# Masked position tables for the sparse attention branch, made by GpSimd ahead of time, in place of mask products on TensorE

## The chip, the cores and the metric

One core of a Trainium2 chip runs the whole kernel in one launch. The metric is device time in microseconds of one execution, the median of several. The engines are TensorE (PE in the rows, with PEld for its weight loads), VectorE (DVE), ScalarE (ACT), GpSimd (POOL) and SyncE (SP, which here only issues DMAs). Each has its own instruction queue that runs in order, and they wait for each other on semaphores.

## The reference, cut to what matters

The kernel computes one decoder layer for 512 tokens of width 1024: a shared input projection, three attention branches whose outputs are merged by gates, an output projection, and a SwiGLU. The change lies in branch A, sparse attention with 8 heads, of which this is the core:

```
score = einsum('bqh,bqhs->bqs', wi, relu(einsum('bqhd,bsd->bqhs', qi, k_idx)))
score = where(key_pos <= q_pos, score, -inf)
_, sel = top_k(score, 128)                      # one choice of keys for all 8 heads
bias = bias_tab[rel_bucket(q_pos - sel)]        # one column per head
logits = q_lat . kv_lat[sel] * ATTN_SCALE + bias
p = softmax(where(dist >= 0, logits, -inf))
```

The kernel gathers nothing. It computes the products with all visible keys and pushes the keys that were not chosen out by a large number. For the first 128 queries every visible key is chosen, so that only the query blocks 1, 2 and 3 (with 256, 384 and 512 keys, together 1152 columns) need a mask.

## The kernel before, in words

**The stages around the change.** An indexer makes `score` [128, 1152]. DVE then takes the 128 largest of each row away in rounds (`select_keys`), and one DVE instruction turns what is left into `key_mask`: 1e30 where a key is not chosen, 0 where it is (line 2042, semaphore `mask_ready`). Behind it comes the attention stage, a hand-written schedule of 88 steps `v`. Steps 0 to 31 are the dilated branch (C), steps 32 to 63 branch A, steps 64 to 79 the differential branch (B). In branch A step v = 32 + 4h + i is head h (0 to 7), query block i (0 to 3), with 128(i+1) keys. The 88 steps are mixed on TensorE with dense projections (`project`, lines 877 to 879, and the `bv` products, lines 1247 to 1249), so that TensorE has work while the other engines turn a step's scores into probabilities.

**One step.** PE writes logits, with the sign turned, into a PSUM bank (`scores`). DVE adds the position table and takes the row minimum in one instruction (`shift`, line 2065, semaphore `shifted`). ACT takes the exponential (line 1605, `exped`). DVE takes the reciprocal of the row sum (line 2083), POOL scales (line 808, `normed`), PE transposes (line 1153), ACT copies (line 1617, `pt_ready`), PE multiplies with the values (lines 1177, 1182, 1185). Steps are begun in pairs: at an even v DVE and PE take v and v+1. PE may only begin the scores of step k once step k-2 is shifted (line 1110), since there are two banks.

**The mask.** The logits of a step of branch A are two products on PE (lines 1128 and 1129) and, for i > 0, a third one: the identity `ident_r` times the columns of `key_mask` of this block, added into the same bank (line 1135).

**The tables.** For each head a table [128, 512] in SBUF holds the bias by distance, with 1e30 where a key lies ahead of the query. It is a Toeplitz read of `rep_dram`, 128 copies of a row in DRAM (`toeplitz`). SP loads them into two buffers `tab[0]` and `tab[1]` in turn (line 670), in its loop over n. The order of SP's queue matters here: at n = 0 and 1 the two tables of heads 0 and 1 are issued one behind the other, and only then `keys_twice(0)` and `keys_twice(1)` (line 654), each two DMAs that copy 64 rows of the keys of a pair of heads into the other 64 partitions. `keys_twice(t)` waits for ACT, which writes the keys of pair t at step KEY_STEPS[t] (26 and 35 for the first two; line 1679). At n = 2 SP first stores and reloads the dilated outputs `o_far` (lines 667 and 669), then loads the table of head 2.

**POOL** has nothing to do between line 802 (`rep_dram`) and step 31.

**ACT** makes `ident_r` at step 24 (line 1662), and the split queries `aq_st` of head pair 0 at steps 24 and 25 (line 1663).

Of the kernel before, what the change touches and what calls it, by code (L numbers as in the profile page):

```python
# [17 lines left out]
F32 = mybir.dt.float32  # L18
# [213 lines left out]
def hybrid_block(nc, a, out):  # L232
# [7 lines left out]
    def sem(name):  # L240
        return ctx.enter_context(nc.semaphore(name))

    with ctx:
# [53 lines left out]
        oc_lo = place("oc_lo", R + 97, [P, 2, S], F32R)  # L297
        o_near = place("o_near", R + 101, [P, NBLK, CW])
        o_far = place("o_far", R + 105, [P, NBLK, CW + 8])
        tab = [place(f"tab{b}", R + 109.25 + 2 * b, [P, S]) for b in range(2)]  # L300
        tab_near = place("tab_near", R + 109.25, [P, C_H, 2 * P])
        tab_far = place("tab_far", R + 113.25, [P, C_H, 2 * P])
        w_ukt = place("w_ukt", R + 25, [P, S])
        ident_r = place("ident_r", R + 16.5, [P, P], F32R)
        key_mask = place("key_mask", R + 12, [P, 1152], F32R)
        va = place("va", R + 57, [P, NBLK, S])
        def pair_stacks(name, places):
            return [[place(f"{name}{j}_{m}", R + at[m], [P, S], F32R) for m in range(2)] for j, at in enumerate(places)]
# [83 lines left out]

        row_dram = nc.dram_tensor("row_flat", [1, FL_W], F32, kind="Internal").ap()
        rep_dram = nc.dram_tensor("row_copies", [P, FL_W], F32, kind="Internal").ap()
        far_dram = nc.dram_tensor("far_rows", [S, CW + 8], F32, kind="Internal").ap()


# [72 lines left out]
        scores_made = sem("scores_made")  # L470
        shifted = sem("shifted")
        exped = sem("exped")
        a_hi_made = sem("a_hi_made")
        a_lo_made = sem("a_lo_made")
        ak_twice = sem("ak_twice")
# [88 lines left out]
        def table_of(v):  # L564

            w = width_of(v)
            if v < MIX_C1:
                return tab_near[:, v % 4, 2 * P - w:2 * P]
            if v < MIX_A:
                return tab_far[:, v % 4, :]  # L570
            return tab[(v // 4) % 2][:, S - w:S]

        w_in = a["w_in"][0]

# [6 lines left out]
        def _(sp):  # L581
# [45 lines left out]
            def branch_cols(name, g):  # L627
                return a[name][0][:, g * CW:(g + 1) * CW].rearrange("(k p) n -> p k n", p=P)

            def toeplitz(f0, pitch, n_rows, w):  # L630

                dims = [[FL_W - 1, P]] + ([[pitch, n_rows]] if n_rows > 1 else []) + [[1, w]]
                return bass.AP(tensor=rep_dram.tensor, offset=f0 + P - 1, ap=dims)

            sp.wait_ge(rows_copied, 16)
            sp.dma_start(tab_near[:], toeplitz(FL_C0, W_C0, C_H, 2 * P)).then_inc(tab_near_in, 16)
            sp.dma_start(tab_far[:, :, 0:P], toeplitz(FL_C1, W_C1, C_H, P)).then_inc(tab_far_in, 16)
# [17 lines left out]

            for n in range(A_H + B_H):

                if n < 2:
                    sp.wait_ge(shifted, MIX_C1)
                elif n - 2 < A_H:  # L660
                    sp.wait_ge(shifted, MIX_A + 4 * (n - 1))
                else:
                    sp.wait_ge(shifted, MIX_B + 8 * (n - 1 - A_H))
                if n == 2:

                    sp.wait_ge(far_packed, 1)
                    sp.dma_start(far_dram.rearrange("(p r) n -> p r n", r=4), o_far[:]).then_inc(far_stored, 16)
                    sp.wait_ge(far_stored, 16)
                    sp.dma_start(o_far[:], far_dram.rearrange("(b p) n -> p b n", p=P)).then_inc(far_in, 16)
                sp.dma_start(tab[n % 2][:], toeplitz(FL_AB + n * W_AB, W_AB, 1, S)).then_inc(tab_in[n % 2], 16)  # L670
                for t in {1: (0, 1), 4: (2,), 5: (3,)}.get(n, ()):
                    keys_twice(t)
                if n == 2:
                    load(21, [(KT, 0, cols(COL_Z + D, CW))])
                if n == 6:
                    load(22, [(KT, 0, cols(COL_Z + 2 * D, CW))])
                if n == 10:
                    load(23, [(4, 0, branch_cols("w_branch_a", 0))])
# [77 lines left out]
        def _(pool):  # L756
# [43 lines left out]
            pool.wait_ge(rows_stored, 16 * 4)  # L800
            pool.wait_ge(w_hi_made[0], 3)
            pool.dma_start(rep_dram, row_dram.to_broadcast([P, FL_W])).then_inc(rows_copied, 16)

            for v in range(MIX_A - 1, MIX_B + 16 + 1):
                if MIX_A <= v - 1 < MIX_B:
# [47 lines left out]
        def _(pe):  # L853
# [251 lines left out]
            def scores(k):  # L1105
# [6 lines left out]
                if v < MIX_C1:  # L1112
                    h = v % 4
                    mm = pe.matmul(ps[:, 0:w], near(0, h)[:, i * P:(i + 1) * P],
                                   near(6, h)[:, (i + 1) * P - w:(i + 1) * P], start=True, stop=True)
                elif v < MIX_A:
                    h, r = v % 4, (v - MIX_C1) // 4
                    for g in range(2):
                        mm = pe.matmul(ps[:, g * P:(g + 1) * P], near(2 + 2 * g, h)[:, r * P:(r + 1) * P],
                                       near(8 + 2 * g, h)[:, r * P:(r + 1) * P], start=True, stop=True)  # L1120
                elif v < MIX_B:
                    t, m = (v - MIX_A) // 8, (v - MIX_A) // 4 % 2
                    if i == 0 and m == 0:
                        pe.wait_ge(a_lo_made, 3 * t + 3)
                        wait_tile_out(pe, ATT_TILE["key", t])
                        pe.wait_ge(ak_twice, 32 * t + 32)
                    q_b = aq_st[pair_of(t)][m][:, i * P:(i + 1) * P]
                    pe.matmul(ps[:, 0:w], q_b, ak_st[pair_of(t)][m][:, 0:w], start=True, stop=False)
                    mm = pe.matmul(ps[:, 0:w], q_b, al_st[pair_of(t)][m][:, 0:w], start=False, stop=i == 0)
                    if i:  # L1130
                        if v == MIX_A + 1:
                            pe.wait_ge(mask_ready, 1)
                            pe.wait_ge(a_hi_made, 3)
                        off = P * i * (i + 1) // 2 - P
                        mm = pe.matmul(ps[:, 0:w], ident_r[:], key_mask[:, off:off + w], start=False, stop=True)
                else:
                    h, m = (v - MIX_B) // 4, k % 2
                    mm = pe.matmul(ps[:, 0:w], bqk[DH * m:DH * m + DH, h, i * P:(i + 1) * P],  # L1138
                                   bqk[DH * m:DH * m + DH, 4 + h, 0:w], start=True, stop=True)
# [308 lines left out]
        def _(act):  # L1448
# [175 lines left out]
            for v in range(N_STEP):  # L1624
# [31 lines left out]
                if query_hi_at(v) is not None:  # L1656
# [2 lines left out]
                    if t:  # L1659
                        act.wait_ge(scores_made, MIX_A + 8 * (max(t, 2) - 2) + (8 if t == 3 else 0))  # L1660
                    if t == 0 and m == 0:
                        act.activation(ident_r[:], ident[:], ACT.Copy)
                    act.activation(aq_st[pair_of(t)][m][rows, :], aq_T[rows, t, :], ACT.Copy).then_inc(a_hi_made, 1)
                for kind, n in latent_tiles_at(v):
                    if kind == "ukt":
# [179 lines left out]
        def _(dve):  # L1845
# [187 lines left out]
            with dve.Fori(0, 3) as i:  # L2033
# [5 lines left out]
            select_keys((1, 2), 72, 16)  # L2039
            make_lo(14)  # L2040
            select_keys((3,), 88, 8)
            dve.tensor_scalar(key_mask[:], score[:], (TAKEN + UNSEEN) / 2, BIG, ALU.is_gt, ALU.mult) \
                .then_inc(mask_ready, 1)


            def shift(k):
# [8 lines left out]
                table = table_of(v)  # L2055
                if MIX_A <= v < MIX_B:
                    h = (v - MIX_A) // 4
                    dve.wait_ge(tab_in[h % 2], 16 * (h // 2 + 1))
                elif v >= MIX_B and v % 4 == 0:
                    h = (v - MIX_B) // 4 + A_H  # L2060
                    dve.wait_ge(tab_in[h % 2], 16 * (h // 2 + 1))
# [418 lines left out]
```

## Time and profile before

| | us |
|---|---|
| median of 3 runs | 989.38 |
| lowest, highest run | 988.29, 989.47 |
| the profiled execution | 987.96 |
| its span in the trace | 986.2 |
| PE busy | 971.9 (99% of the span) |
| DVE busy | 494.0 (50%) |
| ACT busy | 380.7 (39%) |
| POOL busy | 80.2 (8%) |

The profiled execution has 1.8 us around its span. Busy times are sums of instruction durations in which overlapping stretches count once. Matmuls are pipelined, so that the duration of one is longer than the distance from its start to that of the next; the distance is what it costs the engine.

### The profile page before, as it was taken

Reading aid. Unit: us, or ns where it says so; the run is one execution under the profiler, and the core shown is the slowest. Engines: PE = TensorE matmul, PEld = TensorE weight load, DVE = VectorE, ACT = ScalarE, POOL = GpSimd, SP = SyncE. Lnnn points to the kernel's source line nnn. Section 1 sums busy time; section 2 is a strip of 40 time slices with the busy share of each in tenths; the row PEclk is TensorE's granted clock in tenths of the full one; section 3 lists DMA queues with packets and bytes.
Section 4 is the critical chain, followed back from the end, with each engine's and each line's share of the span. In section 5 each row is a group of like instructions: output and inputs, shape, how many; then the busy total and the mean of one; then the engine's idle time right before and its main releaser. Section 6 shows DMA issues by size and latency. Waiting matters only on the chain.

```text
span 986.2 us, 12710 instructions
## 1 busy us (share of the span) xinstructions
PE 971.9 (99%) x4937; PEld 807.2 (82%) x4937; DVE 494.0 (50%) x847; ACT 380.7 (39%) x686; POOL 80.2 (8%) x113
## 2 busy tenths in 40 slices
PE   7999999999999999999999999999999999999997
PEld 4778888878889977888788888988888888888886
DVE  4764778833458556565655555634334334321323
ACT  5355332255578666632222225432222222211322
POOL 1500000000023312100000011000000000000401
PEclk9999999999999999999999999999999999999999
DMA  8742845312223211264646651224443334232412
GB/s 329 239 125 86 265 141 166 111 44 74 87 87 87 76 33 44 66 233 139 213 138 214 245 171 43 71 79 124 142 153 113 106 106 150 86 109 83 129 43 86
DMA packets 88803, 124.18 MB, mean 126 GB/s; under 512 B 4952, under 2 KB 70069, under 8 KB 88626
## 3 DMA queue, kind: packets, MB, share of 16 engines
q1 hardware_dynamic: 88082, 117.03, 36.7%
q0 software_dynamic: 528, 6.22, 2.0%
q8 instruction: 32, 0.52, 0.2%
q10 hardware_dynamic: 144, 0.26, 0.1%
q14 instruction: 17, 0.14, 0.0%
HBM read 119.77 MB, written 8.45 MB: 130 GB/s over the span
## 4 chain that ended last, share of the span: by engine, by line
PE 95%; issue 2%; POOL 1%; DMA 1%; SPq 0%; DVE 0%; ACT 0%; POOLq 0%; DVEq 0%
PE tile_ps L877 19%; PE tile_ps L878 18%; PE tile_ps L879 18%; PE t_ps L1153 2%; PE o_ps L1185 2%; PE tile_ps L1336 1%; PE s_ps L1336 1%; PE t_ps L1336 1%; PE tile_ps L1335 1%; PE s_ps L1335 1%; PE t_ps L1335 1%; PE tile_ps L1334 1%; PE s_ps L1334 1%; PE t_ps L1334 1%; PE s_ps L1138 1%
## 5 line engine op out<-in xcount | busy, mean ns | idle before, releaser
L877 PE MATMUL tile_ps<-h_hi,w_hi 128*128 128x512 f32 x736 | 291.0, 395 | 0.0
L878 PE MATMUL tile_ps<-h_lo,w_hi 128*128 128x512 f32 x736 | 286.9, 390 | 0.0
L879 PE MATMUL tile_ps<-h_hi,w_lo 128*128 128x512 f32 x736 | 286.8, 390 | 0.0
L1861 DVE TENSOR_TENSOR w_lo<-w_raw,w_hi 128x2048 fp32r<-128x2048 f32 (+3 forms) x60 | 130.6, 2176 | 155.8 <-ACT w_hi L1460 154.5
L877 PEld LDWEIGHTS tile_ps<-h_hi,w_hi 128*128 128x128 f32 x736 | 138.1, 188 | 36.1 <-issue 6.9
L879 PEld LDWEIGHTS tile_ps<-h_hi,w_lo 128*128 128x128 f32 x736 | 138.2, 188 | 29.4
L878 PEld LDWEIGHTS tile_ps<-h_lo,w_hi 128*128 128x128 f32 x736 | 138.2, 188 | 27.3 <-issue 0.2
L1460 ACT ACTIVATE w_hi<-w_raw 128x2048 fp32r<-128x2048 f32 (+3 forms) x60 | 107.3, 1788 | 43.8 <-DMA w_raw<-in_w_branch_c_dram 10.8
L1858 DVE TENSOR_TENSOR t_lo<-t_raw,t_hi 128x2048 fp32r<-128x2048 f32 (+1 forms) x15 | 32.8, 2184 | 85.6 <-ACT t_hi L1458 85.5
L1458 ACT ACTIVATE t_hi<-t_raw 128x2048 fp32r<-128x2048 f32 (+1 forms) x15 | 27.0, 1799 | 81.5 <-PE s_ps L1336 53.5
L1605 ACT ACTIVATE nl<-nl,cst 128x256 f32<-128x256 f32 (+3 forms) x81 | 42.6, 527 | 29.8 <-DVE cst L2065 29.5
L1808 ACT ACTIVATE f_hi<-f_t 128x512 f32 (+1 forms) x22 | 13.9, 632 | 88.3 <-DVE f_t L2387 88.3
L2387 DVE TENSOR_TENSOR f_t<-tile_ps,silu_t 128x512 f32<-128x512 f32 x20 | 13.8, 692 | 54.7 <-PE tile_ps L879 54.7
L1802 ACT ACTIVATE silu_t<-tile_ps 128x512 f32<-128x512 f32 x22 | 13.0, 597 | 72.0 <-PE tile_ps L879 72.0
L808 POOL TENSOR_SCALAR nl<-nl,cst 128x128 f32<-128x128 f32 (+3 forms) x32 | 22.6, 710 | 219.8 <-DVE cst L2083 218.8
L1617 ACT ACTIVATE pt<-t_ps 128x128 f32<-128x128 f32 (+2 forms) x80 | 29.5, 407 | 21.0 <-PE t_ps L1153 20.3
L834 POOL TENSOR_TENSOR x<-gated,x 128x512 f32<-128x512 f32 x4 | 5.0, 1287 | 297.2 <-DVE gated L2308 297.2
L2065 DVE CUSTOM_DVE_ANT_0 nl<-s_ps,tab 128x256 f32<-128x256 f32 (+3 forms) x49 | 22.6, 478 | 10.9 <-PE s_ps L1138 4.8
L2226 DVE SCALAR_TENSOR_TENSOR ada_sum<-ada,cst,ada_sum 128x1024 f32<-128x1024 f32 x21 | 26.9, 1283 | 0.7
L2015 DVE MAX8 cst<-score 128x8 f32<-128x256 f32 (+2 forms) x48 | 25.2, 553 | 1.4
L2023 DVE MATCH_REPLACE8 score<-cst,score 128x256 f32<-128x256 f32 (+2 forms) x48 | 25.8, 544 | 0.0
L1153 PE MATMUL t_ps<-ident,nl 128*128 128x128 f32 x160 | 24.4, 274 | 0.0
(412 smaller groups left out, 1665.6 us busy)
## 6 DMA issues: line engine op xcount, KB each, us to landing
w_raw<-in_w_in_dram SPq DMA_DIRECT2D x31, 1024.0 KB, 6.0
w_raw<-in_w_gate_up_dram SPq DMA_DIRECT2D x22, 1024.0 KB, 7.0
ada<-in_w_ada_dram SPq DMA_DIRECT2D x12, 1024.0 KB, 5.7
t_raw<-in_w_down_dram SPq DMA_DIRECT2D x10, 1024.0 KB, 5.0
row_copies<-row_flat POOLq DMA_DIRECT2D x1, 5632.0 KB, 23.0
ada<-in_w_ada_dram SPq DMA_DIRECT2D x8, 640.0 KB, 11.4
ada<-in_w_ada_dram SPq DMA_DIRECT2D x8, 512.0 KB, 4.4
ada<-in_w_ada_dram SPq DMA_DIRECT2D x8, 384.0 KB, 10.1
```

Of the source, the lines that this page charges most:

```text
L877: pe.matmul(dst[0:mw, :], wh, x_hi[:, kx, :], start=start, stop=False)
L878: pe.matmul(dst[0:mw, :], wh, x_lo[:, kx, :], start=False, stop=False)
L879: mm = pe.matmul(dst[0:mw, :], wl, x_hi[:, kx, :], start=False, stop=stop)
L1153: mm = pe.transpose(t_ps[v % 2][:, j * P:(j + 1) * P], src[:, j * P:(j + 1) * P], ident[:])
L1334: pe.matmul(bank[:], x_hi[:, kx, blk], wh[:, kw, :], start=start, stop=False)
L1335: pe.matmul(bank[:], x_hi[:, kx, blk], wl[:, kw, :], start=False, stop=False)
L1336: mm = pe.matmul(bank[:], x_lo[:, kx, blk], wh[:, kw, :], start=False, stop=stop)
L1460: hi = nc.scalar.activation(w_hi[s][:, 0:kt, 0:n_cols], w_raw[s][:, 0:kt, 0:n_cols], ACT.Copy)
L1605: act.activation(b, b, ACT.Exp, bias=negmax[:, k:k + 1], scale=-1.0, accum_out=expsum[:, k:k + 1]).then_inc(exped, 1)
L1617: act.activation(pt[v % 2][:, 0:w], t_ps[v % 2][:, 0:w], ACT.Copy).then_inc(pt_ready, 1)
L1858: dve.tensor_tensor(t_lo[s][:, 0:wide, :], t_raw[s][:, 0:wide, :], t_hi[s][:, 0:wide, :].bitcast(F32), ALU.subtract).then_inc(w_split[s], 1)
L1861: dve.tensor_tensor(w_lo[s][:, 0:kt, 0:n_cols], w_raw[s][:, 0:kt, 0:n_cols], w_hi[s][:, 0:kt, 0:n_cols].bitcast(F32), ALU.subtract) \
```

## The change

POOL adds mask and position table of each of the 8 heads ahead of branch A. It loads the head's plain table into SBUF (`plain_table`), adds the mask of the three blocks to it (three additions of 256, 384 and 512 columns), and stores the sum [128, 1152] in DRAM (`sum_dram`), for one head after the other. This begins once the mask is there and runs while the other engines are in the dilated stage. The mask is written over `score` itself instead of into `key_mask`. PE's third product and `ident_r` go. A table in SBUF is now [128, 128 + 1152]: the plain table of block 0 and the sums of blocks 1 to 3, which SP loads by two DMAs per head, 64 KB and 576 KB, in place of one of 256 KB. `tab[0]` now lies where `score` lay, and `tab[1]` over the tables of the dilated stage.

The waits that go with it: ACT waits at step 24 until the sums of all heads are stored, since `aq_st` lies where POOL keeps its sums; SP waits for the same ahead of the table of head 0; at n = 1 SP issues `keys_twice(0)` and `keys_twice(1)` first, then waits for the end of the dilated stage's shifts (step 31), then loads the table of head 1.

```diff
@@ sync, loop over n
+                for t in {1: (0, 1)}.get(n, ()):
+                    keys_twice(t)
-                if n < 2:
-                    sp.wait_ge(shifted, MIX_C1)
+                if n == 0:
+                    sp.wait_ge(masked_stored, 32 * A_H)
+                elif n == 1:
+                    sp.wait_ge(shifted, MIX_A)
                 elif n - 2 < A_H:
                     sp.wait_ge(shifted, MIX_A + 4 * (n - 1))
...
-                sp.dma_start(tab[n % 2][:], toeplitz(FL_AB + n * W_AB, W_AB, 1, S)).then_inc(tab_in[n % 2], 16)
-                for t in {1: (0, 1), 4: (2,), 5: (3,)}.get(n, ()):
+                if n < A_H:
+                    sp.dma_start(tab[n % 2][:, 0:P], toeplitz(FL_AB + n * W_AB + S - P, W_AB, 1, P)) \
+                        .then_inc(tab_in[n % 2], 16)
+                    sp.dma_start(tab[n % 2][:, P:P + 1152], sum_dram[n]).then_inc(tab_in[n % 2], 16)
+                else:
+                    sp.dma_start(tab[n % 2][:, 0:S], toeplitz(FL_AB + n * W_AB, W_AB, 1, S)).then_inc(tab_in[n % 2], 16)
+                for t in {4: (2,), 5: (3,)}.get(n, ()):
                     keys_twice(t)
@@ gpsimd, behind line 802
+            def plain_table(h):
+                if h >= 2:
+                    pool.wait_ge(masked, h - 1)
+                pool.dma_start(tab_plain[h % 2][:], toeplitz(FL_AB + h * W_AB, W_AB, 1, S)).then_inc(plain_in, 16)
+
+            def masked_table(h):
+                pool.wait_ge(plain_in, 16 * (h + 1))
+                if h + 1 < A_H:
+                    plain_table(h + 1)
+                src = tab_plain[h % 2]
+                for i in range(1, NBLK):
+                    w, off = P * (i + 1), P * i * (i + 1) // 2 - P
+                    dst = tab_sum[h % 2][1][:] if i == 3 else tab_sum[h % 2][0][:, off:off + w]
+                    ins = pool.tensor_tensor(dst, src[:, S - w:S], score[:, off:off + w], ALU.add)
+                ins.then_inc(masked, 1)
+                pool.wait_ge(masked, h + 1)
+                if h:
+                    pool.wait_ge(masked_stored, 32 * h)
+                pool.dma_start(sum_dram[h, :, 0:640], tab_sum[h % 2][0][:]).then_inc(masked_stored, 16)
+                pool.dma_start(sum_dram[h, :, 640:1152], tab_sum[h % 2][1][:]).then_inc(masked_stored, 16)
+
+            pool.wait_ge(rows_copied, 16)
+            pool.wait_ge(mask_ready, 1)
+            plain_table(0)
+            for h in range(A_H):
+                masked_table(h)
@@ tensor, scores
-                    mm = pe.matmul(ps[:, 0:w], q_b, al_st[pair_of(t)][m][:, 0:w], start=False, stop=i == 0)
-                    if i:
-                        if v == MIX_A + 1:
-                            pe.wait_ge(mask_ready, 1)
-                            pe.wait_ge(a_hi_made, 3)
-                        off = P * i * (i + 1) // 2 - P
-                        mm = pe.matmul(ps[:, 0:w], ident_r[:], key_mask[:, off:off + w], start=False, stop=True)
+                    mm = pe.matmul(ps[:, 0:w], q_b, al_st[pair_of(t)][m][:, 0:w], start=False, stop=True)
@@ scalar, step 24
-                        act.activation(ident_r[:], ident[:], ACT.Copy)
+                        act.wait_ge(masked_stored, 32 * A_H)
@@ vector
-            dve.tensor_scalar(key_mask[:], score[:], (TAKEN + UNSEEN) / 2, BIG, ALU.is_gt, ALU.mult) \
+            dve.tensor_scalar(score[:], score[:], (TAKEN + UNSEEN) / 2, BIG, ALU.is_gt, ALU.mult) \
...
-                    dve.wait_ge(tab_in[h % 2], 16 * (h // 2 + 1))
+                    dve.wait_ge(tab_in[h % 2], 32 * (h // 2 + 1))
```

## Rows read from the trace of the kernel before

**Rows 1.** The page: busy time, share of the span, instructions, of the two PE queues.
```profile
PE 971.9 (99%) x4937; PEld 807.2 (82%) x4937; DVE 494.0 (50%) x847; ACT 380.7 (39%) x686; POOL 80.2 (8%) x113
```

**Rows 2.** Stretches: from:to, length, busy PE, PEld, DVE, ACT, POOL, clock, DMA.
```profile
285.00:293.00 8.00, 8.00 (x68) 7.87 (x66) 7.06 (x16) 5.43 (x15) 4.42 (x4) 1.00 0.49 143
...
980.00:983.00 3.00, 0.00 (x0) 0.00 (x0) 1.43 (x3) 1.22 (x3) 0.74 (x2) 1.00 0.21 81
983.00:986.00 3.00, 0.00 (x0) 0.00 (x0) 0.04 (x1) 0.01 (x1) 0.00 (x0) 0.50 0.47 175
```

**Rows 3.** Timeline of PE, head 1: start us, us, engine, line, what, columns.
```profile
288.85 0.34 PE L1135 MATMUL s_ps<-key_mask,ident_r 128*128 128x384 f32 x1
289.02 0.40 PE L1128 MATMUL s_ps<-ak_st,aq_st 128*128 128x512 f32 x1
...
289.49 0.39 PE L1135 MATMUL s_ps<-key_mask,ident_r 128*128 128x512 f32 x1
289.72 0.28 PE L1247 MATMUL tile_ps<-w_hi,h_hi 128*128 128x256 f32 x1
289.84 0.28 PE L1248 MATMUL tile_ps<-w_lo,h_hi 128*128 128x256 f32 x1
```

**Rows 4.** Timeline of DVE where the mask is made.
```profile
197.36 0.76 DVE L2042 TENSOR_SCALAR key_mask<-score 128x1152 fp32r<-128x1152 f32 x1
```

**Rows 5.** Timeline of POOL: a DMA issue, two groups of scalings, an addition pair.
```profile
36.57 0.70 POOL L791 DMA_DIRECT2D gkv<-in_g_kv_dram  x1
...
278.49 0.95 POOL L808 TENSOR_SCALAR nl<-nl,cst 128x128 f32<-128x128 f32 x2 [177.87 <-DVE cst L2083]
...
289.68 2.85 POOL L808 TENSOR_SCALAR nl<-nl,cst 128x128 f32<-128x128 f32 x2 [3.11 <-DVE cst L2083]
...
586.31 2.54 POOL L822 TENSOR_TENSOR x<-gated,x_res 128x512 f32<-128x512 f32 x2 [177.43 <-DVE gated L2308]
```

**Rows 6.** Timeline of ACT at step 24.
```profile
256.56 0.30 ACT L1662 ACTIVATE ident_r<-ident 128x128 fp32r<-128x128 f32 x1
...
259.15 0.66 ACT L1617 ACTIVATE pt<-t_ps 128x256 f32<-128x256 f32 x2
```

**Rows 7.** Timeline of PE: values behind step 24; the scores of step 38; the transposes of steps 36, 37.
```profile
263.66 1.00 PE L1182 MATMUL o_ps<-cv,pt 128*128 128x64 f32 x8
...
288.42 0.42 PE L1128 MATMUL s_ps<-ak_st,aq_st 128*128 128x384 f32 x1
...
292.72 0.49 PE L1153 MATMUL t_ps<-ident,nl 128*128 128x128 f32 x3
```

**Rows 8.** Timeline of SP's queue (DMA issues) around the tables of heads 0 and 1.
```profile
263.43 1.05 SPq L670 DMA_DIRECT2D tab<-row_copies  x2
...
286.14 1.10 SPq L654 DMA_DIRECT2D ak_st<-ak_st  x2
```

**Rows 9.** DMA views: landing of line 670; issues with KB each and us to landing.
```profile
DMA to landing us min/median/max: 2.6/3.5/7.5
```
```profile
o_far<-far_rows SPq DMA_DIRECT2D x1, 528.0 KB, 3.8
...
gkv<-in_g_kv_dram POOLq DMA_DIRECT2D x1, 64.0 KB, 3.9
```

**Rows 10.** Timeline of DVE, steps 36 to 38 (in brackets the idle time before).
```profile
285.47 0.29 DVE L2065 CUSTOM_DVE_ANT_0 nl<-s_ps,tab 128x128 f32<-128x128 f32 x1
...
286.96 0.48 DVE L2102 MEMSET al_st<- 64x512 f32 x1 [0.70 <-ACT ak_st L1679]
...
289.42 0.22 DVE L2083 RECIPROCAL cst<-cst 128x1 f32<-128x1 f32 x2
289.56 2.27 DVE L1861 TENSOR_TENSOR w_lo<-w_raw,w_hi 128x2048 fp32r<-128x2048 f32 x1
291.87 0.56 DVE L2065 CUSTOM_DVE_ANT_0 nl<-s_ps,tab 128x384 f32<-128x384 f32 x1
```

**Rows 11.** Who waited for whom, steps 32 to 63: us in total, times, longest.
```profile
PEld t_ps L1153 <- POOL nl L808: 0.2, 1, 0.2
```

More of the change, by code:

```diff
@@ L299, in hybrid_block @@
         o_far = place("o_far", R + 105, [P, NBLK, CW + 8])
-        tab = [place(f"tab{b}", R + 109.25 + 2 * b, [P, S]) for b in range(2)]
+        tab = [place(f"tab{b}", R + at, [P, P + 1152]) for b, at in enumerate((12, 109.25))]
+        tab_plain = [place(f"tab_plain{b}", R + at, [P, S]) for b, at in enumerate((10, 31))]
+        tab_sum = [[place(f"tab_sum{b}_{j}", R + at[j], [P, w]) for j, w in enumerate((640, S))]
+                   for b, at in enumerate(((93, 98), (95.5, 117.25)))]
         tab_near = place("tab_near", R + 109.25, [P, C_H, 2 * P])
@@ L303, in hybrid_block @@
         w_ukt = place("w_ukt", R + 25, [P, S])
-        ident_r = place("ident_r", R + 16.5, [P, P], F32R)
-        key_mask = place("key_mask", R + 12, [P, 1152], F32R)
         va = place("va", R + 57, [P, NBLK, S])
@@ L394, in hybrid_block @@
         rep_dram = nc.dram_tensor("row_copies", [P, FL_W], F32, kind="Internal").ap()
+        sum_dram = nc.dram_tensor("masked_tables", [A_H, P, 1152], F32, kind="Internal").ap()
         far_dram = nc.dram_tensor("far_rows", [S, CW + 8], F32, kind="Internal").ap()
@@ L472, in hybrid_block @@
         exped = sem("exped")
+        plain_in = sem("plain_in")
+        masked = sem("masked")
+        masked_stored = sem("masked_stored")
         a_hi_made = sem("a_hi_made")
@@ L570, in table_of, with toeplitz @@
                 return tab_far[:, v % 4, :]
-            return tab[(v // 4) % 2][:, S - w:S]
+            if v < MIX_B and w > P:
+                off = P * (w // P - 1) * (w // P) // 2
+                return tab[(v // 4) % 2][:, off:off + w]
+            off = 0 if v < MIX_B else S - w
+            return tab[(v // 4) % 2][:, off:off + w]
+        def toeplitz(f0, pitch, n_rows, w):
+            dims = [[FL_W - 1, P]] + ([[pitch, n_rows]] if n_rows > 1 else []) + [[1, w]]
+            return bass.AP(tensor=rep_dram.tensor, offset=f0 + P - 1, ap=dims)
         w_in = a["w_in"][0]
@@ L628, in branch_cols @@
                 return a[name][0][:, g * CW:(g + 1) * CW].rearrange("(k p) n -> p k n", p=P)
-            def toeplitz(f0, pitch, n_rows, w):
-                dims = [[FL_W - 1, P]] + ([[pitch, n_rows]] if n_rows > 1 else []) + [[1, w]]
-                return bass.AP(tensor=rep_dram.tensor, offset=f0 + P - 1, ap=dims)
             sp.wait_ge(rows_copied, 16)
@@ L2057, in shift @@
                     h = (v - MIX_A) // 4
-                    dve.wait_ge(tab_in[h % 2], 16 * (h // 2 + 1))
+                    dve.wait_ge(tab_in[h % 2], 32 * (h // 2 + 1))
                 elif v >= MIX_B and v % 4 == 0:
                     h = (v - MIX_B) // 4 + A_H
-                    dve.wait_ge(tab_in[h % 2], 16 * (h // 2 + 1))
+                    dve.wait_ge(tab_in[h % 2], 32 * (A_H // 2) + 16 * ((h - A_H) // 2 + 1))
                 b, before = nl_of(k)
```

## The prediction, made before the changed kernel was run

> **What bounds the kernel now.** I read the page first. Its first section says that TensorE is busy for 99% of the span [rows 1]; no other engine comes near. Whatever takes work off PE's queue counts in full, as long as nobody makes PE wait, and whatever makes PE wait counts in full too. The stretches of the attention stage come next: in the 8 us from 285 to 293, where head 1 of branch A begins, PE is never idle and its clock is granted in full, but DVE is busy for 7.06 of 8.00 and POOL for 4.42 [rows 2]. So in just this place two further queues are nearly full. The list of waits for branch A confirms it: PE waits once for another engine, 0.2 us, and that is for POOL's scaling of a step [rows 11]. The reader should see two things: PE sets the time, and around step 38 the chain DVE, POOL, PE has no slack to give.
>
> **What goes.** The 24 mask products (8 heads, blocks 1 to 3). Their cost is the distance to the next start, not their duration: 384 columns 289.02 - 288.85 = 0.17 us, 512 columns 289.72 - 289.49 = 0.23 us, and for 256 columns the distance of two other products of that width, 289.84 - 289.72 = 0.12 us [rows 3]. That is 0.52 us a head, 8 x 0.52 = 4.2 us of PE, all on the path. ACT also loses 0.30 us for `ident_r` [rows 6], hidden by PE. The instruction that makes the mask keeps its size and counts as nothing; DVE's work behind it is the first step of the dilated stage, where its 0.76 us [rows 4] were hidden before and stay so.
>
> **What comes, on POOL.** The mask is there at 197.36 + 0.76 = 198.1 [rows 4]. The first plain table costs an issue of 0.7 us and lands some 3.9 us after its issue began [rows 5, 9]: 202.0. A head then takes one load issue (0.7), three additions over 1152 columns at 2.54 / 2 / 512 = 2.5 ns each, that is 2.9 us [rows 5], two store issues (1.4) and about 0.1 for the wait on its own last addition: 5.1 us. Eight heads, less one load issue, make 40.1: 242.1. The landing of the stores of the head before (3.9 from the issue) is covered by the 4.4 us of work up to the next store. Then there is the meeting with DVE. Two scalings of 128 and 256 columns take POOL 0.95 us when DVE is quiet and 2.85 us beside DVE's 2.27 us weight split: 1.9 us more [rows 5, 10]. Three such splits lie in this time (they start at 205, 221 and 240); I add 3 x 1.9 = 5.7 us, and 3.2 for the last store to land: 251.
>
> The Trainium skill has a rule on this: in "SBUF — State Buffer", section "Who interferes with whom", a DVE instruction with two SBUF inputs and a GpSimd instruction that reads SBUF take turns, whole instruction by whole instruction, and whoever issued first goes first. The trace agrees with its 1.9 us. By that rule the reverse can happen as well, a weight split held up by one addition; then 1.3 us go to DVE instead of 1.9 to POOL, and the same sum ends at 245.
>
> Who waits for this? ACT at step 24, where `ident_r` was, at 256.56 [rows 6], 5.6 us later than 251. If ACT is held, everything behind it is late: the queries, a weight conversion, and the copy of step 24's transposes that ends at 259.81. PE uses that copy at 263.66 [rows 6, 7], so ACT has 3.9 us more before PE feels it. I cost this wait at nothing. Without this cover: if DMAs took the 7.5 us of the slowest table load [rows 9], each head would wait for the stores before it, 8.2 us a head, and the last would land at 206.4 + 7 x 8.2 + 7.5 = 271.3: ACT 14.7 late, PE 10.8. The other bound is no cost.
>
> **What comes, on SP.** SP reaches the tables of heads 0 and 1 only at 263.43 [rows 8], since it sits behind weight loads until then. So the wait for all sums ahead of head 0's table costs nothing, and 64 + 576 KB have until step 32 at 277. Its two extra DMAs put 0.5 us each on SP, ahead of nothing urgent. The table of head 1 is another matter. It was issued at 263.9 and is used at step 36. Now it stands behind `keys_twice(1)`, which waits for ACT's step 35. Those two copies are issued from 286.14 to 287.24 [rows 8]. Yet DVE shifts step 36 at 285.47 [rows 10]: the table cannot even be asked for when it is needed. ACT has no idle time in front of its step 35, so its keys come only about 0.1 us earlier in the new kernel, and the issues run to 287.1. The small load takes 0.5, the large one starts at 287.65. Its landing: the nearest row in size and kind is `o_far`, 528 KB into SBUF in 3.8 us; the bounds are the fastest and the slowest table load of 256 KB, 2.6 and 7.5 [rows 9]. I take 3.8, that is 291.45, and the shift of step 36 at 291.5, 6.0 us late (4.9 to 9.8 by the bounds).
>
> **What that wait holds up.** Behind it on DVE stand step 37's shift, the low halves of the keys of pair 1, the reciprocals of steps 36 and 37 at 289.42, the weight split at 289.56 and the shift of step 38 at 291.87. The only idle time among them is the 0.70 in front of the keys [rows 10]. So from there on DVE is 6.0 - 0.7 = 5.3 us late: reciprocals at 294.7, POOL's scaling (2.85) until 297.7, PE's transposes of steps 36 and 37 at 298.0 in place of 292.72 [rows 7]. PE is held twice. First at the scores of step 38, which need the shift of step 36. Without the hold they would start at 288.42 less the 0.64 us of mask products gone by then, 287.8; now at 291.9: 4.1 us. Then at the transposes: without a second hold at 292.72 - 1.04 + 4.1 = 295.8, now 298.0: 2.2 us. Together 6.3 us. Nothing earns it back, for PE had no idle time before in which to do so. The later tables (each 640 KB, in a window of one head's 8.4 us and what DVE is ahead) are covered: that of head 2, behind `o_far`, should land about 298.5, and its first shift moves from 295.05 to 300.4, late by the same 5.3.
>
> **The sum.** -4.2 + 6.3 = +2.1 us. Against the profiled execution's own time that is 987.96 + 2.1 = 990.1 (span 988.3). The median of the runs shown is 1.4 above that execution, so the median should go from 989.4 to 991.5. With the landing at its bounds, 2.6 and 7.5, the sum is +0.9 and +5.8: 990.3 to 995.2.
>
> **The rivals.**
> *Clock.* PE would stand still for 4.1 us at full clock. After its last product, near 980, the clock stayed full for the next 3 us and is at half (1.2 GHz) in the 3 us behind [rows 2]. So a hold of 4.1 us can bring it down. Between 291.9 and 298.0 PE has 3.9 us of work; at half clock that is 7.8, ending 1.7 us after 298.0, and if the low clock lasts as long again, another 1.7 to 2: about +5.5 in all, 995. For it: the length of the hold. Against it: the row at the end begins after a drain, so that the true delay of the fall may be longer than 4.1 us, and the second hold swallows part of the loss. The Trainium skill, "TensorE: Matmul & The Clock Gate", section "What's actually happening", states that an idle engine falls to the low level; the end of this trace agrees.
>
> *POOL late.* As priced above, if the sums are not stored by 260.5 (256.56 + 3.9), each us counts: up to 2.1 + 10.8, about 1002. For it: 16 stores and 8 loads with descriptors made on POOL itself, beside DVE's work. Against it: 9 us between 251 and 260.5.
>
> *Partly made good.* POOL takes the two scalings before DVE's weight split begins (0.95 in place of 2.85) or SP comes earlier, and the landing is near 2.6: the holds together fall to 4.2, the change is even, 989.4. Break-even is a table that lands at 289.2.
>
> *Faster.* Head 1's table is in time, or the shift of step 36 does not hold PE: then the 4.2 us stay, 985.2. The shift decides it: it costs nothing if the table is there by about 286.2. For it speaks only that I read SP's order from the code; against it that the keys of pair 1 come from PE's product at 284 and that no DMA in the trace of this size lands in under 2.6 us.
>
> **How the numbers follow.** Forecast as summed: 0.52. Clock: 0.11. POOL late: 0.11. Partly made good: 0.14. Faster: 0.12. 0.2% of the time is 2.0 us, about what a measurement of this kernel can tell from no change. The forecast's own range, 990.3 to 995.2, straddles 991.4; as most landings lie by 3 to 4 us and +2.1 is just above the bound, I count 0.31 of its 0.52 as slower and 0.21 as same. Slower: 0.31 + 0.11 + 0.10 = 0.52. Same: 0.21 + 0.13 + 0.01 = 0.35. Faster: 0.12 + 0.01 = 0.13. The range leaves out most of the faster case and the upper half of "POOL late": 986.8 to 996.5. The likeliest case alone is 990.3 to 995.2.
>
> **What the new profile would show.** Line 1135's group is gone and no PE time takes its place. POOL has eight equal groups of three additions after 198 and its last store lands near 251; ACT has no wait at step 24. SP issues `keys_twice(1)` near 286 and the 576 KB load near 287.6. DVE idles some 6 us in front of the shift of step 36, for the DMA of `tab`, and PE some 4 us for that shift and 2 us for POOL. From head 2 on no further wait. The prediction is wrong if there is no DVE wait on `tab` at step 36; if POOL's stage ends after 260; or if PE's holds are followed by a stretch with a granted clock under full.

## The result, and the profile after

The changed kernel takes 992.38 us (median of 9 runs, 991.27 to 993.41) against 989.18 for the kernel before (9 runs, 988.29 to 989.69). The ratio is 1.0036, 95% interval [1.0027, 1.0045]: 2.7 to 4.5 us slower. The forecast was 991.5 within 986.8 to 996.5, with "slower" as the likeliest way. The profiled execution took 993.07 us, its span is 991.3.

The busy times on the page of the changed kernel answer to [rows 1]:

```profile
PE 970.4 (98%) x4913; PEld 804.3 (81%) x4913; DVE 494.8 (50%) x847; ACT 380.1 (38%) x685; POOL 118.0 (12%) x161
```

From the list of PE's waits of the same kernel (us in total, times, longest), the one inside the attention stage:

```profile
PE s_ps L1175 <- DVE cst L2106: 5.1, 1, 5.1
```

PE has 24 products fewer (4913 against 4937), POOL is busy for 38 us more, and there is one hold of PE that was not there before.

SP's queue in the changed kernel, around the end of the dilated stage, answers to [rows 8]:

```profile
288.15 0.58 SPq L684 DMA_DIRECT2D tab<-row_copies  x1
288.78 0.43 SPq L686 DMA_DIRECT2D tab<-masked_tables  x1
289.33 0.36 SPq L680 DMA_DIRECT2D far_rows<-o_far  x1
295.23 0.37 SPq L682 DMA_DIRECT2D o_far<-far_rows  x1
```

The large load of head 1's table is issued at 288.78, as forecast (287.65, and everything in this execution is 1.2 us later from step 0 on, since the first weights, `ada`, landed later).

DVE in the changed kernel, steps 36 to 40, answers to [rows 10]; the bracket is the idle time before and what ended it:

```profile
293.98 0.29 DVE L2106 CUSTOM_DVE_ANT_0 nl<-s_ps,tab 128x128 f32<-128x128 f32 x1 [7.84 <-DMA tab<-masked_tables]
...
297.26 0.22 DVE L2124 RECIPROCAL cst<-cst 128x1 f32<-128x1 f32 x2
297.40 2.27 DVE L1902 TENSOR_TENSOR w_lo<-w_raw,w_hi 128x2048 fp32r<-128x2048 f32 x1
299.70 0.56 DVE L2106 CUSTOM_DVE_ANT_0 nl<-s_ps,tab 128x384 f32<-128x384 f32 x1
...
302.85 0.27 DVE L2106 CUSTOM_DVE_ANT_0 nl<-s_ps,tab 128x128 f32<-128x128 f32 x1
```

This is the wait that was forecast, with its cause in the bracket. DVE is idle for 7.84 us, where some 6 were forecast. The load took 293.98 - 288.78 = 5.2 us, not 3.8. Behind it stand the reciprocals, the weight split and step 38's shift in the forecast order, and at step 40 (302.85) there is no new wait.

PE over the same time, answers to [rows 7], and POOL's scaling of steps 36 and 37, answers to [rows 5]:

```profile
294.34 0.69 PE L1175 MATMUL s_ps<-ak_st,aq_st 128*128 128x384 f32 x1 [5.13 <-DVE cst L2106]
...
299.97 0.89 PE L1194 MATMUL t_ps<-ident,nl 128*128 128x128 f32 x3
300.64 0.30 PE L1175 MATMUL s_ps<-ak_st,aq_st 128*128 128x128 f32 x1
```

```profile
297.52 2.85 POOL L855 TENSOR_SCALAR nl<-nl,cst 128x128 f32<-128x128 f32 x2 [10.32 <-DVE cst L2124]
```

PE stands 5.13 us at step 38. The second hold is inside the 299.97 row: one of the three transposes starts then, the other two wait until POOL is done at 300.37 (the three take 0.67 us to the next start, unhindered ones 0.24). It is short because PE worked at half clock in between, as the stretches of 1 us show (PE busy, PEld, DVE, ACT, POOL, then the granted clock). They answer to [rows 2]:

```profile
293.00:294.00 1.00, 0.00 (x0) 0.00 (x0) 0.02 (x1) 0.00 (x0) 0.00 (x0) 1.00 0.82 336
294.00:295.00 1.00, 0.66 (x2) 0.66 (x3) 0.84 (x5) 0.68 (x3) 0.00 (x0) 0.67 0.19 76
295.00:296.00 1.00, 1.00 (x5) 0.71 (x4) 0.97 (x2) 0.97 (x5) 0.00 (x0) 0.50 0.00 0
...
297.00:298.00 1.00, 1.00 (x8) 1.00 (x7) 0.97 (x4) 0.00 (x0) 0.48 (x1) 0.63 0.86 301
298.00:299.00 1.00, 1.00 (x12) 1.00 (x11) 1.00 (x1) 0.00 (x0) 1.00 (x1) 1.00 1.16 365
```

The next rows show POOL's stage (its start, the three additions of one head, the last store) and ACT at step 24, which answers to [rows 6]:

```profile
199.91 0.57 POOL L826 DMA_DIRECT2D tab_plain<-row_copies  x1 [98.06 <-DVE score L2083]
...
203.73 2.96 POOL L837 TENSOR_TENSOR tab_sum<-tab_plain,score 128x256 f32<-128x256 f32 x3
...
243.34 0.55 POOL L843 DMA_DIRECT2D masked_tables<-tab_sum  x1
```

```profile
257.77 0.62 ACT L1704 ACTIVATE aq_st<-aq_T 64x512 fp32r<-64x512 f32 x1
```

The last store is issued at 243.34 and lands 2.9 us later by the DMA view, at 246.2. ACT's row has no bracket: it did not wait. Two of DVE's three weight splits in this time took longer than the 2.29 us that all three took in the kernel before:

```profile
206.29 2.56 DVE L1902 TENSOR_TENSOR w_lo<-w_raw,w_hi 128x2048 fp32r<-128x2048 f32 x1 [1.51 <-ACT w_hi L1501]
...
241.76 2.89 DVE L1902 TENSOR_TENSOR w_lo<-w_raw,w_hi 128x2048 fp32r<-128x2048 f32 x1
```

**A measure for the experiments.** The distances between the starts of DVE's shifts measure the attention stage best, as they don't depend on when the stage began. These are the first shifts of steps 32 and 64, in the kernel before and in the changed one:

```profile
277.05 0.29 DVE L2065 CUSTOM_DVE_ANT_0 nl<-s_ps,tab 128x128 f32<-128x128 f32 x1 [1.16 <-PE s_ps L1129]
...
344.69 0.27 DVE L2065 CUSTOM_DVE_ANT_0 nlb<-s_ps,tab 128x128 f32<-128x128 f32 x1
```

```profile
278.26 0.29 DVE L2106 CUSTOM_DVE_ANT_0 nl<-s_ps,tab 128x128 f32<-128x128 f32 x1 [1.16 <-PE s_ps L1176]
...
349.72 0.27 DVE L2106 CUSTOM_DVE_ANT_0 nlb<-s_ps,tab 128x128 f32<-128x128 f32 x1
```

The distances in us, from the start of one step's first shift to that of another:

| kernel | 32 to 36 | 36 to 40 | 40 to 64 | 32 to 64 |
|---|---|---|---|---|
| before | 8.42 | 9.58 | 49.64 | 67.64 |
| changed | 15.72 | 8.87 | 46.87 | 71.46 |

The change costs 7.30 us up to step 36, gets back 0.71 up to step 40 (DVE's idle time) and 2.77 over heads 2 to 7: +3.8 in this execution, +3.2 between the medians.

### The profile page after: what moved, and what is told of

Its sections match the earlier page's. It is cut to its first block, busy times and chain, and to the rows that moved or that the text cites. A ratio compares the mean times of both kernels' runs of the same rounds, so it can differ in the third digit from the quotient of the medians.

```text
span 991.3 us, 12730 instructions
## 1 busy us (share of the span) xinstructions
PE 970.4 (98%) x4913; PEld 804.3 (81%) x4913; DVE 494.8 (50%) x847; ACT 380.1 (38%) x685; POOL 118.0 (12%) x161
## 4 chain that ended last, share of the span: by engine, by line
PE 93%; issue 2%; POOL 2%; DMA 1%; ACT 1%; DVE 1%; SPq 0%; POOLq 0%; DVEq 0%
PE tile_ps L924 19%; PE tile_ps L925 18%; PE tile_ps L926 18%; PE t_ps L1194 2%; PE o_ps L1226 2%; PE tile_ps L1377 1%; PE s_ps L1377 1%; PE t_ps L1377 1%; PE tile_ps L1376 1%; PE s_ps L1376 1%; PE t_ps L1376 1%; PE tile_ps L1375 1%; PE s_ps L1375 1%; PE t_ps L1375 1%; PE s_ps L1179 1%
## 5 line engine op out<-in xcount | busy, mean ns | idle before, releaser
L2428 DVE TENSOR_TENSOR f_t<-tile_ps,silu_t 128x512 f32<-128x512 f32 x20 | 13.8, 692 | 54.7 <-PE tile_ps L926 54.7
L869 POOL TENSOR_TENSOR x<-gated,x_res 128x512 f32<-128x512 f32 x4 | 5.1, 1290 | 184.5 <-DVE gated L2349 184.5
```

## The experiments

Each is compared with runs of the kernel before on the same chip (medians 988.4 to 989.2).

**1. Only the order of two things in SP's queue, in the changed kernel.**

```diff
-                for t in {1: (0, 1)}.get(n, ()):
+                for t in {1: (0,)}.get(n, ()):
                     keys_twice(t)
...
-                for t in {4: (2,), 5: (3,)}.get(n, ()):
+                for t in {1: (1,), 4: (2,), 5: (3,)}.get(n, ()):
                     keys_twice(t)
```

> The changed kernel with one move in SP's queue: the table of head 1 is loaded ahead of the key copies of head pair 1, not behind them. Theory A (the loss is the wait of step 36 on this table and what it holds up): the table is asked for near 274 and lands near 280, DVE does not wait at step 36, and the 4.2 us of mask products are won: 985.0 us, ratio to before 0.996 (984 to 986). Rival B (the loss comes from the larger tables, from the DMA traffic or from GpSimd's additions beside DVE): the move changes little, 990 to 993. Rival C (clock): goes with A here.

Measured: 987.45 us, ratio 0.9987 [0.9978, 0.9996]. The sign turns: this kernel is faster than the one before, by 1.2 us, and by the ratios it is 4.9 us better than with SP's queue as it was. The wait at step 36 is gone. Yet it is 2.4 us short of the 985.0 of theory A. The waits and SP's queue of this kernel tell why:

```profile
DVE nl L2106 <- DMA tab<-masked_tables: 2.6, 1, 2.6
```

```profile
287.84 0.52 SPq L680 DMA_DIRECT2D far_rows<-o_far  x1
290.87 0.38 SPq L682 DMA_DIRECT2D o_far<-far_rows  x1
291.28 0.51 SPq L684 DMA_DIRECT2D tab<-row_copies  x1
292.21 0.32 SPq L686 DMA_DIRECT2D tab<-masked_tables  x1
```

The table of head 2 stands behind the store and the reload of the dilated outputs. It is issued at 292.21 and used at step 40, where DVE now waits 2.6 us for it (until 298.16) and PE 1.6. The load takes 5.8 us, with a weight load of 1024 KB issued 0.4 us behind it. The distances are 7.89 from 32 to 36, then 12.39 from 36 to 40. In the changed kernel this second wait was covered by the first.

**2. The same order put into the kernel before, with nothing else of the change.**

```diff
             for n in range(A_H + B_H):
+                for t in {1: (0, 1)}.get(n, ()):
+                    keys_twice(t)
...
-                for t in {1: (0, 1), 4: (2,), 5: (3,)}.get(n, ()):
+                for t in {4: (2,), 5: (3,)}.get(n, ()):
```

> The kernel before with the one move in SP's queue that the change makes, and nothing else: both key copies ahead of the (still plain, 256 KB) table of head 1. Theory A: the table is issued near 287.2 and lands some 3.5 us later, DVE shifts step 36 near 290.8, 5.3 us late, 4.6 after its idle time: 993.8 us (992.5 to 995), ratio near 1.0047. Rival B (size of the tables, or GpSimd's stage): no more than 990.

Measured: 992.83 us, ratio 1.0038 [1.0024, 1.0052], that is 4.2 us between the medians; 4.6 was expected. DVE's shift of step 36:

```profile
291.45 0.29 DVE L2067 CUSTOM_DVE_ANT_0 nl<-s_ps,tab 128x128 f32<-128x128 f32 x1 [5.14 <-DMA tab<-row_copies]
```

13.54 us from step 32 to 36 instead of 8.42: 5.1 late, 5.3 expected. The order alone, with small plain tables and no work on POOL, makes at least as large a loss as the whole change (4.2 against 3.2 us).

**3. POOL's stage alone, in the kernel before.** The diff adds `plain_table` and `masked_table` as in the change, their buffers and semaphores, and ACT's wait:

```diff
                         act.activation(ident_r[:], ident[:], ACT.Copy)
+                        act.wait_ge(masked_stored, 32 * A_H)
```

> The kernel before with GpSimd's stage added (eight plain tables loaded, 24 additions, 16 stores) and ACT's wait for it at step 24; nobody reads the sums, and the mask products and plain tables stay. Theory A: GpSimd is done near 247, ACT does not wait: 989.2 us, within 0.5 of before. Rival B (the stage costs through DMA traffic, through DVE's weight splits that have to wait, or through ACT's wait): 990.5 or more.

Measured: 988.80 us, ratio 1.0002 [0.9993, 1.0011]; from step 32 to 64 it takes 67.62 us, before 67.64. POOL's 37 us of work and its 6.8 MB of additional traffic, laid over the dilated stage, cost nothing that can be seen; rival B's 990.5 lies outside the interval.

**4. The mask products alone taken out of the kernel before.**

```diff
-                    mm = pe.matmul(..., start=False, stop=i == 0)
+                    mm = pe.matmul(..., start=False, stop=True)
...
-                        off = P * i * (i + 1) // 2 - P
-                        mm = pe.matmul(ps[:, 0:w], ident_r[:], key_mask[:, off:off + w], start=False, stop=True)
```

> The kernel before without the 24 mask products; the choice of the 128 keys is left out of the result, nothing else. Theory A (a product costs the distance to the next start, 0.12, 0.17 and 0.23 us): 4.2 us less, 985.0. Rival D (PE's time comes back as waits for DVE or POOL, which are nearly as busy there): 987 to 989. Rival E (a product costs its whole duration, 24 x 0.338 = 8.1 us): 981.

The result of this kernel leaves out the choice of the 128 keys. Measured: 985.84 us, ratio 0.9972 [0.9963, 0.9981], 2.8 us less; 4.2 lies outside the interval (1.9 to 3.7). Between the two: theory A's price with some of rival D. From step 32 to 64 it takes 64.54 us, 3.1 less than before. By heads: 7.92 us from 32 to 36 (8.42 before, the 0.5 is won), but 9.92 from 36 to 40 (9.58 before, lost again), and 8.68 from 48 to 52 (8.69 before, nothing won). In the other heads 0.4 to 1.1 is won. From step 36 to 40, where DVE and POOL set the pace [experiment 10], a shorter queue on PE gives nothing. What sets it at head 4 no run tests: there ACT is the next fullest engine (8.23 of 8.70 us without the products, 7.91 before), POOL is not (2.65).

**5. PE kept at work in its hold, in the changed kernel.**

```diff
+                if v == MIX_A + 6:
+                    pe.wait_ge(o_read[1], 4)
+                    for _ in range(17):
+                        pe.matmul(o_ps[1][:], h_hi[:, 0, 0:P], h_hi[:, 0, :], start=True, stop=True)
                 if k >= 2:
                     pe.wait_ge(shifted, k - 1)
```

> The changed kernel, with 17 products of 512 columns put in front of the scores of step 38, where TensorE stands still for 5.1 us: some 3.9 us of work whose result nobody reads (it goes to a bank that is free there). It tells what the clock costs, which fell to half at 294 in the changed kernel and rose near 297.7. Theory A (the fall is swallowed, since what comes next is held by DVE and GpSimd anyway): the clock stays full, TensorE's second hold, in front of the transposes, grows from about 0.5 to some 2 us, and the time stays: ratio to before 1.0036 as for the changed kernel, within 0.0006. Theory C (the clock costs its 1.8 us): ratio 1.0018.

Measured: 992.83 us, ratio 1.0035 [1.0021, 1.0048]. The stretch from 293 to 301 of this kernel (0.79 was the granted clock of that stretch in the changed kernel), and the transposes of step 36:

```profile
293.00:301.00 8.00, 5.97 (x38) 4.68 (x36) 5.41 (x11) 2.25 (x7) 2.17 (x1) 1.00 0.68 231
```

```profile
301.28 0.89 PE L1198 MATMUL t_ps<-ident,nl 128*128 128x128 f32 x3 [0.93 <-POOL nl L855]
```

The clock stays full and the time is the same. PE arrives earlier at the transposes and waits there for POOL, 0.93 us in front of the first and some 0.4 more in front of the two others (the three take 0.66 us to the next start, unhindered ones 0.24). That is 1.3 us where 2 were expected; another 0.35 goes to a wait for ACT at 297. The distance from 36 to 40 is 8.87 as in the changed kernel. The interval leaves out the 1.0018 of theory C, if only just, and the unchanged distance says the same: in that kernel the low clock cost nothing.

**6. How long may POOL take?** Both kernels start from that of experiment 1. In the first, each addition of 512 columns is made twice:

```diff
+                    if i == 3:
+                        pool.tensor_tensor(dst, src[:, S - w:S], score[:, off:off + w], ALU.add).then_inc(masked, 1)
+                        pool.wait_ge(masked, 2 * h + 1)
                     ins = pool.tensor_tensor(dst, src[:, S - w:S], score[:, off:off + w], ALU.add)
```

> The kernel with head 1's table ahead of the key copies (987.45 us, ratio 0.9987), in which GpSimd makes each addition of 512 columns twice. Its stage grows by 8 x (1.3 + 0.3) = 13 us, its last store lands near 259.4 in place of 246.6, while ACT asks for it at 257.4. By my reckoning TensorE feels ACT only 3.9 us after that, at 261.3: no loss, 987.5. Rival (ACT's hold counts from its first us): 989.

Measured: 988.58 us, ratio 0.9992 [0.9983, 1.0001], against 0.9987 [0.9978, 0.9996] without the additional work: no difference that the intervals allow to tell. The last store is issued at 255.35 and lands 2.8 us later, at 258.15; ACT takes up step 24's queries at 258.25 without waiting. The stage grew by some 12 us, and its reserve of about 11 is used up, but ACT was not held, so that neither the 3.9 us behind it nor the rival was tried by this kernel.

**7. All 24 additions made twice**, by the same edit for every i.

> The same with all 24 additions made twice: the stage grows by 8 x (2.9 + 0.9) = 30 us, the last store lands near 277, ACT stands 20 us at step 24, TensorE 16 less or more: 987.5 + 15.7 = 1003 us (1000 to 1006). Rival (there is more cover than I count, or the later steps catch up): under 998.

Measured: 1004.28 us, ratio 1.0152 [1.0136, 1.0167]. With experiment 1's ratio that is 0.0165 x 989 = 16.3 us more; 15.7 was expected. The waits of this kernel, ACT for the stores and PE for ACT:

```profile
ACT aq_st L1706 <- DMA masked_tables<-tab_sum: 18.2, 1, 18.2
...
PE o_ps L1225 <- ACT pt L1660: 13.8, 1, 13.8
```

ACT stands 18.2 us and PE 13.8, so that 4.4 us are covered (3.9 reckoned). The expectation had 20 and 16: its total came out close partly by luck, since a cost that it did not count makes up for the shorter hold. From step 0 to step 32 the kernel takes 94.8 us instead of 77.9, 16.9 more. The 3.1 us beyond PE's wait are probably the half clock behind it: PE works at it from 279.1 to about 285.8, and half of these 6.7 us is 3.3 (an estimate; no run keeps the clock up here to test it).

```profile
262.00:266.00 4.00, 3.33 (x13) 2.06 (x11) 0.00 (x0) 0.00 (x0) 3.62 (x4) 1.00 0.00 0
266.00:270.00 4.00, 0.00 (x0) 0.00 (x0) 0.00 (x0) 0.00 (x0) 3.83 (x6) 0.84 0.39 147
...
278.00:282.00 4.00, 2.89 (x14) 2.56 (x14) 3.66 (x7) 3.93 (x10) 0.00 (x0) 0.50 0.00 0
282.00:286.00 4.00, 4.00 (x16) 3.15 (x16) 3.30 (x9) 2.05 (x7) 0.00 (x0) 0.53 0.96 296
```

**8. The store of the dilated outputs moved as well.** Experiment 1's kernel, with the store issued ahead of the key copies of pair 1:

```diff
+                if n == 1:
+                    sp.wait_ge(far_packed, 1)
+                    sp.dma_start(far_dram.rearrange("(p r) n -> p r n", r=4), o_far[:]).then_inc(far_stored, 16)
                 for t in {1: (1,), 4: (2,), 5: (3,)}.get(n, ()):
                     keys_twice(t)
...
                 if n == 2:
-                    sp.wait_ge(far_packed, 1)
-                    sp.dma_start(far_dram.rearrange("(p r) n -> p r n", r=4), o_far[:]).then_inc(far_stored, 16)
                     sp.wait_ge(far_stored, 16)
```

> The kernel with head 1's table ahead of the key copies, and also with the store of the dilated outputs ahead of the key copies of head pair 1, so that their reload and the table of head 2 are issued some 2.5 us earlier. In the run before, DVE waited 2.6 us and TensorE 1.6 us at step 40 for the table of head 2. Theory A (that wait is what stands between this kernel and the one without mask products): the table lands near 295, no wait or one under 0.5 us at step 40, ratio 0.9972 as without the products: 985.8 us. Rival B (what is left is the cost of the larger tables or of GpSimd's stage): ratio 0.9985.

Measured: 985.88 us, ratio 0.9964 [0.9951, 0.9978]. SP's queue of this kernel:

```profile
284.85 0.32 SPq L689 DMA_DIRECT2D far_rows<-o_far  x1
286.55 1.11 SPq L663 DMA_DIRECT2D ak_st<-ak_st  x2
287.76 0.53 SPq L680 DMA_DIRECT2D o_far<-far_rows  x1
288.34 0.55 SPq L682 DMA_DIRECT2D tab<-row_copies  x1
289.31 0.32 SPq L684 DMA_DIRECT2D tab<-masked_tables  x1
```

The table of head 2 is asked for 2.9 us earlier, and DVE waits for no table any more. From step 32 to 64 it takes 64.51 us; the kernel without mask products took 64.54. So the larger tables and POOL's stage are free once both issues are moved, and what the change can win is won: 3.1 us against the kernel before. Against the changed kernel it is 6.3 us, each measured against its own baseline (-3.1 and +3.2).

**9. The table of head 1 alone in flight**, in the changed kernel:

```diff
                     sp.wait_ge(far_packed, 1)
+                    sp.wait_ge(tab_in[1], 32)
                     sp.dma_start(far_dram.rearrange("(p r) n -> p r n", r=4), o_far[:]).then_inc(far_stored, 16)
```

> The changed kernel, with the store of the dilated outputs held back until the table of head 1 has landed. In the changed kernel that 528 KB store is issued 0.55 us behind the 576 KB load, which took 5.2 us, where I had reckoned 3.8. If the company of the store is the cause, the load now takes 3.8 to 4.1 us, and DVE shifts step 36 1.1 to 1.4 us earlier; the store, the reload and the table of head 2 come later in turn, and DVE waits at step 40 instead, so that the time is no better: 992 to 995. If it is the load itself (its rows, or the key copies ahead of it), it takes 4.9 to 5.2 again.

The DMA view of this kernel, for the issues from 288 to 290 (KB, us to landing):

```profile
tab<-masked_tables SPq DMA_DIRECT2D x1, 576.0 KB, 3.9
```

The load takes 3.9 us alone, 5.2 with the store beside it. The store paid as well in the changed kernel (3.0 us in the kernel before):

```profile
far_rows<-o_far SPq DMA_DIRECT2D x1, 528.0 KB, 5.9
```

DVE shifts step 36 14.50 us behind step 32 instead of 15.72. The expected new wait at step 40 did not come (from 36 to 40 it takes 8.87 us, as before the edit): head 2's table was issued at 296.4 and used at 301.3. From 32 to 64 it takes 70.54 instead of 71.46; the measured time, 992.06 us, ratio 1.0039 [1.0024, 1.0053], cannot tell so little.

**10. DVE's weight split moved one step back**, from step 37 to 38, in experiment 8's kernel:

```diff
-    return {2: 15, 10: 16, 18: 17, 26: 18, MIX_A + 5: 19, MIX_A + 21: 20, Z_STEPS[0] + 2: 21, Z_STEPS[2] + 4: 22,
+    return {2: 15, 10: 16, 18: 17, 26: 18, MIX_A + 6: 19, MIX_A + 21: 20, Z_STEPS[0] + 2: 21, Z_STEPS[2] + 4: 22,
```

> The version with both moves in SP's queue (985.88 us, ratio 0.9964), and also with DVE's 2.3 us weight split moved from step 37, right behind the reciprocals of steps 36 and 37, to step 38, behind the shifts of 38 and 39. Without the mask products the first shifts of steps 36 and 40 lie 9.9 us apart (9.6 with them): what head 0 and head 1 win on TensorE, 0.9 us, is given back there. Theory A (DVE's split holds up GpSimd's scaling, 2.85 us in place of 0.95, and the shift of step 38, and with them TensorE): the distance falls to 9.1 and the time by 0.8: ratio 0.9956. Rival D (something else sets the distance, such as ACT or the key copies): distance 9.6 or more, ratio 0.9964 as before.

POOL's scaling of steps 36 and 37 in this kernel:

```profile
290.09 0.82 POOL L856 TENSOR_SCALAR nl<-nl,cst 128x128 f32<-128x128 f32 x2 [3.33 <-DVE cst L2125]
```

0.82 us instead of 2.85: the long duration was the meeting with DVE's split. The distance from 36 to 40 falls from 9.70 to 8.37. But 0.85 of these 1.33 us come back from 40 to 44 (8.47 in place of 7.62), and from 32 to 64 there is 0.45 us left. The time, 985.23 us, ratio 0.9967 [0.9955, 0.9979], is not to be told from experiment 8's; the interval just holds the 0.9956 of theory A too. Theory A was right about the cause of the distance; of the 0.8 us in the time that it expected, the distances show about half.

## Why the prediction was right, point by point

- **Direction and mechanism: right, and shown.** Head 1's table behind the key copies, a wait of DVE at step 36, two holds of PE. Experiment 1 takes the order out of the change and its sign turns; experiment 2 puts the order alone into the kernel before and makes the loss. That the forecast said "slower" and not "same" was close: its +2.1 stood 0.1 above the bound of 2.0. The measured loss is clear of it because the two terms that were mis-sized both missed to the same side.
- **The landing of the 576 KB load: too small, 3.8 for 5.2 us.** This is the mis-sized term of the sum. I took the row of `o_far` and overlooked that the next thing in SP's queue, the store of 528 KB, shares the DMA engines with the load. Alone it takes 3.9 us [experiment 9]. The shift of step 36 was 7.3 us late, not 6.0.
- **What stands behind it on DVE: right.** 6.0 - 0.7 was the form; 7.30 - 0.71 = 6.6 at step 40 was measured. PE's two holds were forecast at 4.1 and 2.2 us; 5.13 and some 0.4 were measured, and work at half clock fills the time between.
- **The mask products: 4.2 us was too much.** Their price on PE was read rightly, but 0.9 of it is given back from step 36 to 40 and 0.5 at head 4. What remains is 3.1 us in branch A and 2.8 in the time [experiment 4]. I had seen that the first of these stretches had no slack on DVE and POOL, and had not applied it to the gain. The sum should have read -2.8 or -3.1.
- **The sum: +2.1, measured +3.2.** The forecast sum lies below the interval (2.7 to 4.5). The landing accounts for 1.3 of the difference and the products after step 40 for 0.35 (2.77 for 3.12); together that makes the +3.8 of the profiled execution.
- **POOL's stage: right that it is hidden, too long by 5 to 6 us.** It ended at 246.2, 1.2 us of which is this execution's late start; forecast 251. A head took 4.9 us unhindered, 5.1 summed. I had charged 1.9 us three times for the meetings with DVE's splits. Only one head had its additions stretched (3.48 for 2.93 us); in the other two meetings DVE was held, 0.3 and 0.6 us, which is the reverse that the prediction had allowed for. Its sum for that case, 245, is what the late start leaves of 246.2, but partly by luck: twice POOL waited for the stores of the head before, 0.8 and 1.35 us, which the sum had as covered.
- **ACT's reserve: right.** 3.9 reckoned, 4.4 found [experiment 7].
- **Head 2's table covered: right only because of the hold.** In the changed kernel there is no wait at step 40. Without the hold there is one of 2.6 us [experiment 1]. I had said that it is used at 300.4 and lands at 298.5, and not what that means once the first wait is mended.
- **The clock: a sign of being wrong that came true.** The prediction called itself wrong if PE's holds were followed by a granted clock under full. They were: 0.50 from 295 to 296. So it was wrong that the clock stays up behind this hold, and the time came out near only because the fall cost nothing, as what came next was held by DVE and POOL [experiment 5]; the second hold shrank in its place. The Trainium skill, "TensorE: Matmul & The Clock Gate", section "What's actually happening", states that an idle TensorE falls to the low level; this trace agrees.
- **The rivals.** The 995 of the clock rival needed the fall to cost time. POOL was not late. "Partly made good" needed a table that landed by 289.2; it landed at 294. The case "faster" needed an order in SP's queue that wasn't there; made by hand, it comes to 985.9 us, where the rival had 985.2.
- **DVE and POOL taking turns.** POOL's scaling takes 2.85 us beside DVE's split and 0.82 with the split moved away [experiment 10]. In the changed kernel's POOL stage it went either way. Twice a split was issued while an addition ran, and took 0.3 and 0.6 us longer; once the split was first, and a head's additions took 0.55 us longer. This agrees with the rule in the Trainium skill, "SBUF — State Buffer", section "Who interferes with whom", that the one issued first goes first.

## What to carry to other kernels

A change that takes work off the bounding engine can also reorder queues that nobody looks at; read the new queue of the DMA issuer line by line, and ask of each load what it now stands behind and at what time its user wants it. Here one order of two issues cost 4 to 5 us, more than the whole change could win, and with two issues moved the change wins 3.1 us. Where one late load hides another, mending the first shows the second, so work both out before the run. And a gain on the bounding engine counts only in stretches where the others have slack.

## What the runs showed of the hardware that was not expected

- The granted clock fell after holds of different lengths. PE's last product before the hold ended near 289.2 in the changed kernel and the clock fell near 294.3, 5.1 us later. In experiment 2 PE was idle from about 289.5 and the clock fell between 291 and 292, after a hold of only 2.3 us:

```profile
290.00:291.00 1.00, 0.00 (x0) 0.00 (x0) 0.00 (x0) 0.00 (x0) 0.00 (x0) 1.00 0.89 344
291.00:292.00 1.00, 0.20 (x1) 0.20 (x2) 0.55 (x3) 0.22 (x1) 0.00 (x0) 0.93 0.93 380
292.00:293.00 1.00, 1.00 (x4) 1.00 (x5) 0.82 (x4) 0.98 (x5) 0.00 (x0) 0.50 0.05 17
```

- In experiment 7 it fell near 268.7, some 3.4 us after PE's work ended, and in experiment 1 a hold of 1.6 us left it full. The fall cost nothing that can be seen behind the hold at step 38, where DVE and POOL set what followed [experiment 5]. Behind the one at step 24 some 3 us are unexplained otherwise [experiment 7]; that PE sets the pace there, and that this makes the difference, is not shown.
- The store of 528 KB beside the 576 KB load took 5.9 us instead of the 3.0 of the kernel before (2.7 alone in experiment 9), and the load 5.2 instead of 3.9: each pays for the other.
- A DVE instruction and a POOL instruction that meet can stretch either one: DVE's weight split took 2.56 and 2.89 us instead of 2.29 beside POOL's additions, and a head's additions 3.48 instead of 2.93 beside the split between them.
